# RMS norms of a two-layer diffusion trunk on one core: squares folded in the residual stage, token sums on partitions, affine part on ScalarE, tile pairs made in step with weight slabs

## The reference

```python
def _rms(x, g):
    xf = x.astype(jnp.float32)
    y = xf * lax.rsqrt(jnp.mean(xf * xf, axis=-1, keepdims=True) + EPS)
    return (y * g.astype(jnp.float32)).astype(x.dtype)

def _modulate(x, g, shift, scale):
    return _rms(x, g) * (1 + scale) + shift
...
# each layer l (0 even, 1 odd), for both streams of tokens:
#   x = x + gate1 * (mixer(_modulate(x, norm1_g, shift1, scale1)) @ w_out)
#   x = x + gate2 * conv_ffn(_modulate(x, norm2_g, shift2, scale2))
# at the end: y = _rms(x, final_norm_g)
```

## Time and profile before

| | |
|---|---|
| time, median of 3 executions | 2898.34 us (2896.32 to 2904.95) |
| the profiled execution, own time | 2901.56 us |
| its span, first to last instruction | 2899.8 us |
| mean granted TensorE clock in it | 0.934 |
| PE / PEld / DVE / ACT busy | 91% / 82% / 53% / 42% of the span |
| DMA | 608.33 MB, mean 210 GB/s |

### The profile page before, as it was taken

How to read it: one execution, slowest core, us unless ns; L and a number is a source line. 1 busy time by engine, 2 the same in 40 slices (tenths; PEclk the granted TensorE clock), 3 DMA queues, 4 the chain that set the end, 5 groups by cost and what they waited for, 6 DMA issues and landing times. The chain is left out here.

```text
span 2899.8 us, 52317 instructions
## 1 busy us (share of the span) xinstructions
PE 2652.1 (91%) x20832; PEld 2384.0 (82%) x20832; DVE 1527.8 (53%) x1848; ACT 1221.2 (42%) x1488; POOL 0.5 (0%) x6
## 2 busy tenths in 40 slices
PE   6699956979999999999979998667979999999997
PEld 1388945868888888899978895565979999999996
DVE  0533345465545555476675342433575565657666
ACT  0233312324444444465544343132345555556553
POOL 0000000000000000000000000000000000000000
PEclk9899967989999999999989996686989999999998
DMA  9688700667888887865538861021535555555552
GB/s 389 261 315 309 301 18 0 262 232 290 308 316 306 312 319 302 319 233 189 189 109 316 318 204 45 17 90 36 188 124 187 185 189 187 188 189 189 184 194 82
DMA packets 171543, 608.33 MB, mean 210 GB/s; under 512 B 18680, under 2 KB 26872, under 8 KB 171128
## 3 DMA queue, kind: packets, MB, share of 16 engines
q1 hardware_dynamic: 170872, 603.12, 57.5%
q10 hardware_dynamic: 512, 2.97, 0.3%
HBM read 601.38 MB, written 4.63 MB: 209 GB/s over the span
## 5 line engine op out<-in xcount | busy, mean ns | idle before, releaser
L438 DVE TENSOR_TENSOR w_lo<-raw,w_hi 128x1024 fp32r<-128x1024 f32 x756 | 919.9, 1224 | 1010.7 <-ACT w_hi L431 1005.0
L431 ACT ACTIVATE w_hi<-raw 128x1024 fp32r<-128x1024 f32 x756 | 796.7, 1058 | 1146.5 <-PE banks L564 555.4
L562 PE MATMUL banks<-xs_ffn,w_hi 128*128 128x256 f32 x4224 | 1187.9, 281 | 15.6 <-DVE xs_ffn L699 14.7
L563 PE MATMUL banks<-xs_ffn,w_hi 128*128 128x256 f32 x4224 | 1180.4, 279 | 0.0
L564 PE MATMUL banks<-xs_ffn,w_lo 128*128 128x256 f32 x4224 | 1180.2, 279 | 0.0
L562 PEld LDWEIGHTS banks<-xs_ffn,w_hi 128*128 128x128 f32 x4224 | 796.2, 188 | 54.4 <-issue 29.0
L563 PEld LDWEIGHTS banks<-xs_ffn,w_hi 128*128 128x128 f32 x4224 | 796.4, 189 | 0.0
L564 PEld LDWEIGHTS banks<-xs_ffn,w_lo 128*128 128x128 f32 x4224 | 796.1, 188 | 0.0
L524 PE MATMUL banks<-raw,cond 128*32 128x512 f32 x1536 | 219.4, 604 | 28.4 <-PEq L594 17.2
L562 PE MATMUL banks<-xs_odd,w_hi 128*128 128x256 f32 (+2 forms) x640 | 181.9, 284 | 7.1 <-DVE xs_odd L699 7.1
L563 PE MATMUL banks<-xs_odd,w_hi 128*128 128x256 f32 (+2 forms) x640 | 179.9, 281 | 0.0
(11 more groups left out here) (275 smaller groups left out, 2390.7 us busy)
## 6 DMA issues: line engine op xcount, KB each, us to landing
raw<-in_w_mod SPq DMA_DIRECT2D x384, 512.0 KB, 5.8
raw<-in_ffn_w_up SPq DMA_DIRECT2D x352, 512.0 KB, 6.0
raw<-in_ffn_w_down SPq DMA_DIRECT2D x176, 512.0 KB, 3.8
raw<-in_even_w_in SPq DMA_DIRECT2D x72, 512.0 KB, 8.4
raw<-in_odd_w_in SPq DMA_DIRECT2D x64, 512.0 KB, 8.7
raw<-in_even_w_out SPq DMA_DIRECT2D x32, 512.0 KB, 8.7
raw<-in_odd_w_out SPq DMA_DIRECT2D x32, 512.0 KB, 4.2
raw<-in_odd_w_tail SPq DMA_DIRECT2D x8, 448.0 KB, 3.8
```

The lines of the kernel that those rows point to most:

```text
L431: act.activation(w_hi[:, o % SPLIT], raw[:, s % RAW], ACT.Copy).then_inc(hi_done.sem, 1)
L438: dve.tensor_tensor(w_lo[:, o % SPLIT], raw[:, s % RAW], w_hi[:, o % SPLIT].bitcast(F32), ALU.subtract).then_inc(lo_done.sem, 1)
L562: pe.matmul(made, hi, x_hi, start=start and not second, stop=False, skip_group_check=second)
L563: pe.matmul(made, hi, x_lo, start=False, stop=False, skip_group_check=second)
```

## The change

1. **Running squares.** In the residual stages each half group (2 tiles) is now gated and added to `x` at once (`add_half`), ACT squares the half right away (`square_half`), and one slab later DVE folds the squares into a running [128, 256] tile `sums` (`fold_half`: two tiles to one, then onto `sums`). For the first norm this is done for all of `x` at the head of the mod stage. An empty Sqrt on ACT in the first group of a residual stage loads the root's table.
2. **Sums with tokens on partitions.** PE takes the 128 tokens of a stream of `sums` as the stationary operand and two columns of ones as the moving one, so the sum comes out with tokens on partitions, [128, 2] for both streams. Scale, root and reciprocal run on [128, 2] instead of [128, 256]. PE then multiplies this column, repeated 128 times, with the identity, which puts 1/rms for 256 tokens on every partition, in PSUM bank 6; DVE reads it there.
3. **Affine on ScalarE.** Gain and shift are applied by ACT (`Identity` with scale and bias from [128, 1] columns), four [128, 128] instructions for a pair of tiles, where DVE did them.
4. **Pairs in step with slabs.** `xs` is made in 8 pairs of tiles. Three pairs are made ahead of the stream, but for the low part of the third; each later one is made by `act_at` and `dve_at` just ahead of a weight split, in the first pass over the slabs. PE waits for the low part of the pair that it needs.
5. The last norm uses the same sums. To free banks, the rows and columns of the mod products share a bank; a mod group now waits until the group two before it is done (`mod_done`) and not only copied out. At the start POOL clears a [128, 1] tile. `resid_skip` and some small tiles go.

```diff
-        def split_stream(eng, f, split, places, also=None, left=()):
+        def split_stream(eng, f, split, places, also=None, left=(), beside=None):
...
                     if kind == "mod":
                         continue
+                    if beside and first:
+                        beside(eng, f.own_at.index(s))
                     ahead = f.own_at.index(s) + SPLIT
...
             if k == 0:
-                wait(pe, rows_out.sem, f.mod_group(i, j) - 1)
+                wait(pe, mod_done.sem, f.mod_group(i, j) - 1)
...
+        PARTS, LEAD = KD // CHUNKS, 3
...
+            def on_pe(pe):
+                pe.wait_ge(folded.sem, folded.at(0))
+                for st in range(2):
+                    mm = pe.matmul(banks[:, SUM_BANK, 2 * st:2 * st + 2], sums[:, T * st:T * st + T],
+                                   const[:, C_ONES:C_ONES + 2], start=True, stop=True)
+                mm.then_inc(norm_summed.sem, 1)
+                pe.wait_ge(norm_inv.sem, norm_inv.at(1))
+                for st in range(2):
+                    mm = pe.matmul(banks[:, SPREAD_BANK, T * st:T * st + T], over(rt[:, st], P), ident,
+                                   start=True, stop=True)
+                mm.then_inc(norm_spread.sem, 1)
...
+            def modulate(act, b):
+                act.wait_ge(normed.sem, normed.at(b + 1))
+                for k in range(CHUNKS * b, CHUNKS * b + CHUNKS):
+                    for st in range(2):
+                        tile = h[:, k, T * st:T * st + T]
+                        made = act.activation(tile, tile, ACT.Identity, bias=shifts[:, k, st:st + 1],
+                                              scale=gains[:, k, st:st + 1])
+                made.then_inc(modulated.sem, 1)
+                act.wait_ge(modulated.sem, modulated.at(b + 1))
+                act.activation(xs[:, tiles(b), 0:NT], h[:, tiles(b)], ACT.Copy).then_inc(xs_hi.sem, 1)
+
+            def multiply(dve, b):
+                dve.tensor_tensor(h[:, tiles(b)], x[:, tiles(b)],
+                                  banks[:, SPREAD_BANK, 0:NT].unsqueeze(1).broadcast_to([P, CHUNKS, NT]), ALU.mult
+                                  ).then_inc(normed.sem, 1)
+
+            def low(dve, b):
+                dve.wait_ge(xs_hi.sem, xs_hi.at(b + 1))
+                dve.tensor_tensor(xs[:, tiles(b), NT:2 * NT], h[:, tiles(b)], xs[:, tiles(b), 0:NT].bitcast(F32),
+                                  ALU.subtract).then_inc(xs_lo.sem, 1)
...
+            def act_at(act, o):
+                if o + LEAD < PARTS:
+                    modulate(act, o + LEAD)
+
+            def dve_at(dve, o):
+                if o + LEAD < PARTS:
+                    multiply(dve, o + LEAD)
+                if o + LEAD <= PARTS:
+                    low(dve, o + LEAD - 1)
...
+        def square_half(act, sq, q, n):
+
+            act.wait_ge(resid.sem, resid.at(2 * q + n + 1))
+            if q:
+                act.wait_ge(folded.sem, folded.at(2 * q + n - 1))
+            act.activation(sq[:, 2 * n:2 * n + 2], x[:, GROUP * q + 2 * n:GROUP * q + 2 * n + 2], ACT.Square
+                           ).then_inc(squared.sem, 1)
...
+            def add_half(dve, f, i, g, n):
+                q = i * f.groups + g
+                products_done(dve, f, i, g, n)
+                if q:
+                    dve.wait_ge(resid.sem, resid.at(2 * q + n - 1))
+                tiles = slice(GROUP * q + 2 * n, GROUP * q + 2 * n + 2)
+                two = tb[:, 2 * n:2 * n + 2].rearrange("p t (s n) -> p t s n", s=2)
+                made = banks[:, f.first_bank(g) + n, :].rearrange("p (t s n) -> p t s n", t=2, s=2)
+                dve.tensor_tensor(two, made, over(gate[:, tiles, :], T), ALU.mult).then_inc(summed.sem, 1)
+                dve.wait_ge(summed.sem, 2 * f.group(i, g) + n + 1)
+                dve.tensor_tensor(x[:, tiles], x[:, tiles], tb[:, 2 * n:2 * n + 2], ALU.add).then_inc(resid.sem, 1)
...
+            return [square], [add, fold]
```

More of the change, by code:

```diff
@@ L657, in norm_before @@
[L657 to L667, removed]
-            def on_act(act):
[L670 to L682, removed]
+            sum_pe, sum_act, sum_dve = inverse_norm()
+            def tiles(b):
+                return slice(CHUNKS * b, CHUNKS * b + CHUNKS)
+            def modulate(act, b):
[8 more added lines that the diff above has]
+                act.activation(xs[:, tiles(b), 0:NT], h[:, tiles(b)], ACT.Copy).then_inc(xs_hi.sem, 1)
@@ L684, in on_dve @@
+            def on_act(act):
+                sum_act(act)
+                for b in range(LEAD):
+                    modulate(act, b)
             def on_dve(dve):
[L685 to L688, removed]
                 dve.scalar_tensor_tensor(gains, scales, 1.0, over(gain, 2), ALU.add, ALU.mult)
-                dve.wait_ge(E.sem, E.at(1))
@@ L692, in on_dve @@
[L692 to L707, removed]
-                            ts = dve.tensor_scalar(tile, tile, gains[:, k, st:st + 1], shifts[:, k, st:st + 1],
-                                                   ALU.mult, ALU.add)
-                    ts.then_inc(V.sem, 1)
-                    if b:
-                        low(b - 1)
@@ L713, in on_dve @@
-                low(len(PARTS) - 1)
-            def ready(pe, k):
-                b = max(n for n, (k0, _) in enumerate(PARTS) if k0 <= CHUNKS * k)
-                pe.wait_ge(V.sem, V.at(SPLIT_UP[b]))
-            return dict(act=on_act, pe=on_pe, dve=on_dve, steps=(10, 21, 1), ready=ready)
+                sum_dve(dve)
+                for b in range(LEAD):
+                    multiply(dve, b)
+                    if b:
+                        low(dve, b - 1)
+            def act_at(act, o):
+                if o + LEAD < PARTS:
+                    modulate(act, o + LEAD)
@@ L777, in _ @@
                                             also=also(moving[1]),
-                                            left=left)
+                                            left=left, beside=None if n else before.get("act_at"))
                     for _, call in left:
@@ L807, in project @@
                 counted.advance(n)
+            if "over" in before:
+                before["over"]()
         def group_used(f, i, g):
@@ new lines, in residual_pieces, with add, fold, square @@
+        def residual_pieces(tb, sq, gate):
+            def add_half(dve, f, i, g, n):
[9 more added lines that the diff above has]
+                dve.tensor_tensor(x[:, tiles], x[:, tiles], tb[:, 2 * n:2 * n + 2], ALU.add).then_inc(resid.sem, 1)
+            def add(dve, f, i, g):
+                for n in range(2):
+                    add_half(dve, f, i, g, n)
+            def fold(dve, f, i, g):
+                for n in range(2):
+                    fold_half(dve, sq, i * f.groups + g, n)
+            def square(act, f, i, g):
+                if i == 0 and g == 0:
+                    act.activation(spare[:], const[:, C_ONES:C_ONES + 1], ACT.Sqrt)
+                for n in range(2):
+                    square_half(act, sq, i * f.groups + g, n)
+            return [square], [add, fold]
@@ L886, in convolution, with first_squares, first_folds @@
             return [take, None, middle], [None, None, None, neighbour(0), None, neighbour(2)]
-        project([ph["mod"]], [None], [[]], [[]])
+        with ExitStack() as scope:
+            sq = sb("sq", [P, GROUP, NT], scope=scope)
+            def first_squares(act):
+                for q in range(KD // GROUP):
+                    for n in range(2):
+                        square_half(act, sq, q, n)
+            def first_folds(dve):
+                for q in range(KD // GROUP):
+                    for n in range(2):
+                        fold_half(dve, sq, q, n)
+            project([ph["mod"]], [None], [[]], [[]], before=dict(act=first_squares, dve=first_folds))
+            squares_over()
         def ffn(l):
```

146 lines of the change are left out of this document (79 added, 67 removed).

## The result

The changed kernel takes 2936.18 us (median of four, 2935.00 to 2936.85), against 2898.34 before: the ratio is 1.0126, with a 95% interval of 1.0109 to 1.0144. It is 38 us slower, where 2885 was forecast. The norms themselves came out as forecast.

The account below looks back on a forecast made before the run. PE was taken as always busy between norms, with a wait of some 17 us at five norms. Gains of 17.1 us less 4 for the clock made 13, so 2885 us; range 2880 to 2889.5, chance 0.56.

Parts of the forecast that it names:

- the rest costs nothing: Residual stages, mod groups' later wait and POOL's clear: no cost, since three split slabs cover the later splits.
- a slab of 24 matmuls takes 2.80 us: Inside the stages: PE's time for each slab, read from the distance of two `w_lo`, PE always busy at full clock.
- Release: Barrier's end at each norm: even unchanged, the others 3.3, 3.9, 3.3 and 1.1 us later, from squares and folds.
- Release to first multiply: The sum at each norm: 3.3 us instead of 12.45, bounds 2.7 and 5.7; spread product 1.3 of it.
- Slab 7's end from release: Four inner norms: 39.1 us, as 3.3 plus 35.8, with exchange steps of 5.15 us for each slab.
- Gains: Five norms: even 5.1, FFN 0 1.2, odd 1.8, FFN 1 1.0, last norm 8.0 us; together 17.1.
- The clock's 4 us: Slab 7 and those behind it at four norms: PE's lower clock costs 1 us each, 4 in all.
- rival A: Clock falls in each norm's exchange and stays down over slab 7: 3 us each, 2893; chance 0.20 together with D.
- rival C: Residual stages make PE wait for late splits at 12 groups: 2907, or 2915 with 2.5 us each; chance 0.06.
- B, a cheaper exchange: Four affines in 1.17 us give 15 in all, 2870, half of it 2877; chance 0.13 (dear side, 2899, 0.05).
- the 4 us for each norm: Affine left on DVE: each pair 0.53 us cheaper, 4 us for each norm of eight pairs.

Follow-up runs that it names:

- the changed kernel with the shift of 1024: Changed kernel with `rt` and `spare` inside `lam`'s 32 bytes, so later tiles shift by 1024 bytes instead of 1088: 2879.69 us, ratio 0.9929.
- b_w16: Kernel before with both halves of the split weights in one tile, 16 bytes into it, `xs` staying at 32 by 128: 2954.24 us.

## Why the prediction was wrong

**The step that failed** is "the rest costs nothing", and under it the first part's "a slab of 24 matmuls takes 2.80 us", which every later number took as fixed. The pace is not a property of the matmul's shape alone: the same instructions take 2.88 when the new small tiles move one operand by 64 bytes, and over 744 slabs that is the 60 us which the sum didn't have. None of the rivals held this, so 2936 lay outside the range, on a side given 0.06. A run would not have been needed to suspect it: the list of new persistent tiles is in the diff, and all `xs` lie behind them. That the pace depends on it could not be read from one trace, since there every stage has the same distance. The Trainium skill, "SBUF — State Buffer", Operand start alignment, asks of an operand's start only that it be a multiple of its element size, and says that this is about legality and not about speed. Both positions here satisfy it, and the pace differs by 2.9% (2.88 to 2.80).

**The terms of the sum**, measured in the changed kernel with the shift of 1024, in which PE keeps its 2.80. The residual pieces and the last norm there:

```profile
1474.66 0.68 DVE L911 TENSOR_TENSOR tb<-banks,mod 128x512 f32<-128x512 f32 x1
...
1481.43 0.42 DVE L899 TENSOR_TENSOR sums<-sums,sq 128x256 f32<-128x256 f32 x1
1482.19 0.19 DVE L740 SCALAR_TENSOR_TENSOR norm_gain<-mod,par 128x32 f32<-128x32 f32 x1 [0.33 <-PEq L809]
...
1485.11 1.28 DVE L725 TENSOR_TENSOR prj<-x,banks 128x512 f32<-128x512 f32 x2 [1.31 <-PE banks L678]
```

```profile
2862.29 0.69 DVE L911 TENSOR_TENSOR tb<-banks,mod 128x512 f32<-128x512 f32 x1
...
2868.55 6.36 DVE L1940 SCALAR_TENSOR_TENSOR y_out<-x,par,banks 128x256 f32<-128x256 f32 x16 [1.31 <-PE banks L678]
```

- Release: 7.5 us after the odd stage's last pieces start (1474.66 to 1482.19). The forecast had 1492.3 - 1484.75 = 7.55. FFN 0 7.8 against 8.0, FFN 1 7.5 against 7.6.
- Release to first multiply: 2.9 against 3.3. From the start of the two-column products to the instruction that reads them it is 1.0 us (1.25 in the sum), for the spread product 1.3, as taken; the whole is still above the lower bound, 2.7.
- Slab 7's end from release: 39.2 (even, 104.81 to 143.99) and 39.1 in FFN 0 and odd (621.02 to 660.13, 1482.19 to 1521.32), against 39.1.
- Gains, each from the start of the stage's last pieces to slab 7's end, before less now, with before from the earlier trace rows: even 4.7 (5.1 forecast), FFN 0 48.3 - 46.9 = 1.4 (1.2), odd 48.5 - 46.7 = 1.8 (1.8), FFN 1 47.7 - 46.7 = 1.0 (1.0), last norm 14.7 - 6.3 = 8.4 (8.0). Sum 17.3 against 17.1.
- The clock's 4 us: hardly paid. The exchange's stretch in the even norm and the one behind it:

```profile
131.00:144.00 13.00, 10.51 (x74) 9.97 (x74) 6.74 (x8) 8.63 (x15) 0.00 (x0) 0.87 0.61 239
144.00:160.00 16.00, 16.00 (x136) 12.99 (x136) 5.04 (x5) 6.38 (x7) 0.00 (x0) 1.00 0.73 265
```

The clock fell to 0.87 on the mean (the same in FFN 0, 0.91 in FFN 1, 1.00 in odd). That fell on slab 6, where, as worked out, the exchange's next step covers it. From slab 7's first product to the mod products it took 3.0 us, where slab 3 took 2.9, and behind it the clock is 1.00. So rival A, a clock that stays down, falls, and the term of 1 us for each norm should have been 0.2 at the most. The gains above have this cost in them, so no 4 us come off, and that is the main reason why the schedule gave 18.6 and not 13 (20 by the ratio; the fifteen executions of the kernel before alone lie 12 us apart, 2896.13 to 2908.58, so what is left above the 17.3 can't be placed).
- The residual stages (rival C, the only slower one): PE's idle time ahead of the FFN products is put down to `xs` alone in after, so no split was late. C falls; it was on the right side for the wrong reason.
- B, a cheaper exchange: falls, with 1.65 for four affines, as the slope of the copies had it. The estimate from the figures of the Trainium skill's "ScalarE: Activation LUTs", What ACT_TABLE_LOAD costs, was 1.64, and the trace agrees with 1.65. The four affines on DVE took 1.12, but the 4 us for each norm that the prediction gives for leaving them there came to 1.0 to 2.4, since the low part of the first pair then stands behind more of DVE's own work. The rule of the skill's "VectorE: DVE Perf Modes", The perf-mode tier table, that a float32 `tensor_scalar` runs at twice the rate of a `tensor_tensor`, agrees roughly with this trace where both have 2048 columns, 1287 against 2293 ns:

```profile
L1126 DVE TENSOR_SCALAR mix<-mix,par 128x2048 f32<-128x2048 f32 x1 | 1.3, 1287 | 0.0
L1154 DVE TENSOR_TENSOR qkv<-qkv,work 128x2048 f32<-128x2048 f32 x1 | 2.3, 2293 | 0.0
```

## To carry over

A diff's new tiles are part of its cost: list what they shift and compare the operands' places in SBUF, by 128 bytes, before and after; if the pace of a stage that nobody edited moves, pad by 64 bytes first and look at the matmul count of a fixed stretch. In this kernel a pad could have hidden a good schedule or sold a bad one: compare versions at equal operand distances. And where two engines hand work to and fro, make the first link one item ahead, and put nothing ready behind a wait for a load.

## What was not expected of the hardware

With PE never waiting and the clock at 1.00, 256 columns in fp32r took 116.6 ns (400/3431) at a distance of 32 bytes by 128 between the moving operand and the weights, 117.7 at 64, 118.6 at 0, and 119.9 at 96 and at 16. By the two groups above, the products that read the high half of `xs` lost about 4 ns of their mean each, and that of its low half 2. In `b_w16`, at the same pace, all three lost 4 (285, 284 and 283 ns), so 96 and 16 need not have one cause. A shift of 64 bytes is worth 1.9% of this kernel's time, nearly three times what the schedule of the five norms is (0.7%).
